# A hand-written order of tiles in a transformer block: key and value tiles in pairs, modulation tiles between them in runs of eight

## What is computed

```python
mod = silu(c) @ w_ada + b_ada            # the same with c_ctx for the context: six parts of 2048
h  = rmsnorm(x,  norm1_g) * (1 + sc1)  + sh1
hc = rmsnorm(xc, norm1_g) * (1 + csc1) + csh1
k, v   = h  @ w_in[:, K], h  @ w_in[:, V]     # K, V: 512 columns each
kc, vc = hc @ w_in[:, K], hc @ w_in[:, V]
```

## Time and profile before

| | |
|---|---|
| median of three runs | 1503.29 us |
| the profiled execution | 1502.79 us, span 1501.0 us |
| PE busy | 1467.9 us (98%) |
| DVE, ACT, POOL busy | 992.7, 666.2, 49.9 us |
| DMA | 355.73 MB, mean 237 GB/s |
| PE share of the chain that ended last | 86% |
| first 40 us | PE busy 21.72 us, DMA 371 GB/s |

### The profile page before, as it was taken

The page is one execution under the profiler, slowest core; times in us unless marked ns, Lnnn a source line. Parts: engine busy times, 40 slices in busy tenths (PEclk is TensorE's granted clock), DMA queues, the critical chain, the costliest instruction groups (busy, mean ns, idle before and its releaser), DMA issues.

```text
span 1501.0 us, 19363 instructions
## 1 busy us (share of the span) xinstructions
PE 1467.9 (98%) x7297; PEld 1208.5 (81%) x7297; DVE 992.7 (66%) x1166; ACT 666.2 (44%) x900; POOL 49.9 (3%) x32
## 2 busy tenths in 40 slices
PE   5999999999999999999999999999999999999997
PEld 2567888888888788888888888888888888888886
DVE  2456866867667679988776577777655554555456
ACT  3423444565454553344454444444444444444443
POOL 0000000101000000010100000001200000000000
PEclk9999999999999999999999999999999999999999
DMA  9997776755667679889665578778556655555552
GB/s 370 380 353 255 263 260 206 226 187 161 233 197 240 209 230 362 324 297 358 235 209 158 178 239 299 270 272 305 185 169 210 196 191 191 191 195 196 190 192 94
DMA packets 123037, 355.73 MB, mean 237 GB/s; under 512 B 10962, under 2 KB 11986, under 8 KB 122322
## 3 DMA queue, kind: packets, MB, share of 16 engines
q1 hardware_dynamic: 121492, 353.43, 69.0%
q10 hardware_dynamic: 1472, 1.31, 0.3%
HBM read 352.60 MB, written 2.10 MB: 236 GB/s over the span
## 4 chain that ended last, share of the span: by engine, by line
PE 86%; DVE 6%; issue 3%; ACT 3%; DMA 2%; ACTq 0%; POOL 0%; POOLq 0%; SPq 0%; DVEq 0%
PE bank L1546 20%; PE bank L1548 20%; PE bank L1547 20%; PE bank L1832 14%; PE bank L1835 7%; DVE wl L1116 2%; PE bank L1702 2%; PE bank L1675 1%; ACT wh L692 1%; DMA raw<-in_w_ada 1%; DVE acc L1147 1%; PE bank L1665 1%; DMA ident<-in_identity 1%; PE bank L1577 1%; DVE mx L1239 0%
## 5 line engine op out<-in xcount | busy, mean ns | idle before, releaser
L1116 DVE TENSOR_TENSOR wl<-raw,wh 128x1024 fp32r<-128x1024 f32 x451 | 555.5, 1243 | 369.1 <-ACT wh L692 367.6
L692 ACT ACTIVATE wh<-raw 128x1024 fp32r<-128x1024 f32 x452 | 473.2, 1060 | 476.3 <-PE bank L1548 282.8
L1832 PE MATMUL bank<-h2S,wh 128*128 128x512 f32 x896 | 244.8, 394 | 0.8 <-DVE wl L1116 0.7
L1546 PE MATMUL bank<-wh,hT 128*128 128x512 f32 x512 | 206.5, 403 | 1.6 <-DVE wl L1116 1.0
L1548 PE MATMUL bank<-wh,hT 128*128 128x512 f32 x512 | 200.0, 391 | 0.0
L1547 PE MATMUL bank<-wl,hT 128*128 128x512 f32 x512 | 199.7, 390 | 0.0
L1548 PE MATMUL bank<-wh,hidS 128*128 128x512 f32 x496 | 193.0, 389 | 0.0
L1547 PE MATMUL bank<-wl,hidS 128*128 128x512 f32 x496 | 193.0, 389 | 0.0
L1546 PE MATMUL bank<-wh,hidS 128*128 128x512 f32 x496 | 192.9, 389 | 0.0
L1832 PEld LDWEIGHTS bank<-h2S,wh 128*128 128x128 f32 x896 | 153.2, 188 | 21.6 <-DVE wl L1116 0.9
L1147 DVE SCALAR_TENSOR_TENSOR acc<-raw,cc,acc 128x1024 f32<-128x1024 f32 x120 | 153.5, 1279 | 0.0
(11 more groups left out here) (223 smaller groups left out, 1587.7 us busy)
## 6 DMA issues: line engine op xcount, KB each, us to landing
raw<-in_w SPq DMA_DIRECT2D x256, 512.0 KB, 3.7
raw<-in_w_ada SPq DMA_DIRECT2D x192, 512.0 KB, 5.7
raw<-in_w_in SPq DMA_DIRECT2D x128, 512.0 KB, 4.6
raw<-in_w_attn_o SPq DMA_DIRECT2D x32, 512.0 KB, 6.2
raw<-in_w_out SPq DMA_DIRECT2D x32, 512.0 KB, 5.4
raw<-in_w_fourier SPq DMA_DIRECT2D x16, 512.0 KB, 6.8
xt<-in_x SPq DMA_DIRECT2D x2, 1024.0 KB, 6.1
ct<-in_ctx SPq DMA_DIRECT2D x2, 1024.0 KB, 10.5
```

Source lines behind the costliest of these rows:

```text
L692: nc.scalar.activation(slot, raw[:, s % RAW, :], ACT.Copy).then_inc(wh_done, 1)
L1116: nc.vector.tensor_tensor(lo, raw[:, s % RAW, :], hi.bitcast(F32), ALU.subtract)\
L1546: nc.tensor.matmul(bank[b][:], a_hi, w_hi, start=first, stop=False)
L1832: nc.tensor.matmul(out[:].rearrange("p (v t) -> p v t", v=2), wh[:, slot, cols_f[f]], h2S[:, :, block, :], start=(block == 0), stop=False)
```

## The change

Seven of the sixteen entries of one table differ, the third to the ninth:

```diff
-KV_BEHIND = [18, 22, 26, 34, 36, 40, 44, 50, 52, 56, 64, 64, 64, 64, 64, 64]
+KV_BEHIND = [18, 22, 30, 30, 38, 38, 46, 46, 54, 56, 64, 64, 64, 64, 64, 64]
```

## The result

The kernel after the change takes 1507.15 us (median of ten runs, 1506.80 to 1508.27); the kernel before, on the same chip, takes 1503.35 us (ten runs, 1502.83 to 1504.27). The ratio is 1.0027 [1.0018, 1.0036], 3.8 us slower. The forecast was 1506.4 us, in a range of 1503.9 to 1508.2 us. The profiled execution of the new kernel took 1507.13 us, its span 1505.3 us, against 1502.79 and 1501.0 us of the kernel before.

What follows compares the result with a forecast made beforehand. Loads bound the first stage up to 69 us, PE after. +3.18 - 1.98 + 2 x 1.43 - 0.43 - 0.6 + 0.1 = +3.1 us on 1502.79, plus 0.5 to the median: 1506.4 us, range 1503.9 to 1508.2 us.

Steps and rivals of the forecast that it cites:

- The bound: First stage of the kernel before: bound by loads up to 69 us and by PE after it.
- run three: Eight M tiles between K1,1 and V1,0, transposes in the middle: 1.85 + 0.58 + 1.85 = 4.3 us, to 94.4 us.
- Holds at K1,0 and K2,0: PE waits for `modulate(2)` and `modulate(4)` behind the M tiles: 3.86 us chain, 2.43 us cover, 1.43 us each.
- The first run's load wait: Eight M tiles behind K0,1: PE waits 3.2 us for loads, 1.98 us before; V0,0 starts at 62.2 us.
- load 38: S2,1 before, found by PE at 67.99 us; counting five loads back put the first run's last tile at 61.2 us.
- Waits at K1,1: None expected: `modulate(3)` ready at 83 us, K1,1 wants it at 84.6 us; bounds 0 to 1.3 us.
- The sum: All legs from K0,1's end to the C3 tiles: +3.1 us, their start at 123.6 us against 120.53 us before.
- Loads late as well: Rival, 0.20: K1,1 or the eighth tile of run three or four also waits for loads; 1507.4 to 1508.4 us.
- Given back later: Rival, 0.10: a DVE backlog in the query part swallows the 3 us; not slower, 1503.3 to 1503.9 us.
- Only the runs count: Rival, 0.08: holds covered, leaving 1.0 us for three runs fewer and perhaps 2 us load wait; 1500.3 to 1502.3 us.
- the two marks of line 1079: Sign: K1,0 and K2,0 each start about 1.4 us after the last M tile, released by DVE's `hT` row.

Runs made afterwards that it cites:

- e1: Changed kernel with the transposes of S1 and S2 one tile earlier, behind four tiles of their run and not five; 1507.07 us, ratio 1.0026.
- e2: Changed kernel with V0,1 and V1,1 back behind the transposes of C1 and C2, K1 still a pair; 1504.30 us, ratio 1.0008.
- e3: Changed kernel with two M tiles in place of four between the transposes and K1,0, and the same at K2,0; 1508.81 us, ratio 1.0041.
- e4: Changed kernel with V0,0 back behind four M tiles, so the first run of eight is two of four; 1504.41 us, ratio 1.0009.
- e5: e1 with ACT's four small loads moved behind the first C3 tiles and DVE's tables into K3; 1506.72 us, ratio 1.0023.
- e6: Changed kernel with the small loads and tables moved as in e5, the odd cut left in; 1507.74 us, ratio 1.0030.
- e8: Kernel before with K1,1 moved beside K1,0 behind two M tiles and the transposes of S2 one tile earlier; 1504.08 us, ratio 1.0005.
- e9: Kernel before with K1 as the only pair, behind four M tiles, and cuts at even tiles; 1502.88 us, ratio 0.9996.
- e12: Kernel before with K1 and K2 as pairs, cuts even, and half of each S and C load from S1 on left out; 1501.49 us, ratio 0.9988.

## Why the prediction was right, point by point

**The bound.** Right but for one place. The stage waits for loads up to about 62 us now, and PE or the two holds set the pace behind it; but in run three the last tiles land so late that they would have set it, had the odd cut not (e1). All of the change's cost is inside the stage and arrives at the end.

**Holds at K1,0 and K2,0.** Forecast 2 x 1.43 us, measured 2 x 1.34. The difference is the step from DVE to PE: I had taken 0.14 us from an "issue" piece of the chain, and K1,0 starts 0.06 us behind the low half (79.36 to 79.42 us). e2 removes the holds and is faster by 2.9 us, e3 takes two tiles of cover from each and loses 1.7 us. This is shown.

**The first run's load wait.** Forecast V0,0 at 62.2 us, measured 62.69 us; the run took 7.04 us for 6.75. Its last tile could start at 61.71 in place of 61.2 us. The count back from load 38 was right for the kernel before, where the load at this place in the queue landed at 61.2 us (issued at 52.4, 8.8 us to land). In the new kernel's execution it was issued at 52.6 us and took 9.0 us: the first 0.2 us stood there before the change begins, the rest is not explained. e4 takes the wait away; forecast from the same arithmetic at 1504.6 us, it came out at 1504.41 us. Shown.

**Waits at K1,1.** V1,0 was issued at 74.89 us and landed 4.07 us later (forecast 4.0), the high half of `modulate(3)` started at 82.10 us, the low half ended at 83.5 us (forecast 83), and K1,1 began at 85.0 us with no wait. The small loads cost `modulate(3)` nothing that PE saw.

**Run three.** Wrong by 0.84 us, the one step that was mis-sized: "1.85 + 0.58 + 1.85 = 4.3 us". I had split eight tiles evenly, though the transposes stand behind the third tile of any kind after S. In the kernel before, K1,1 is one of those three, and the cut came out even; now all three are tiles of C, which makes five and three: 20 records, the transposes, 12. The rule I had read from the earlier trace rows, 0.86 us for two tiles, holds for whole pairs only. And I had counted the small loads at nothing (at 1 us in the rival), while they make the last tile of the run land 2.5 us later (94.3 in e1, 91.8 in e5; my count was 90.6). The 2 x 2 runs (e1, e5, e6) show that either is enough.

**The sum.** +3.1 us forecast, +4.22 us in the profiled execution: 0.84 us run three, 0.29 us first run, 0.23 us already there ahead of the change, less 0.17 us at the holds and 0.08 us at K/V tiles. The medians differ by 3.8 us. The error of 0.75 us in the time is smaller than the 1.1 us of the sum, and that is luck: the new kernel's profiled execution lay at its median, while I had added 0.5 us for the distance between the two. The holds and the first run's wait, which carry the sum, were forecast for the right reason.

**The rivals.** *Loads late as well* was true in part: not at K1,1, but the tiles of run three (e1 shows it), hidden behind the odd cut. *Given back later* is refuted: the delay is 4.22 us at V2,1 and 4.14 to 4.16 us up to 1062 us. *Only the runs count* is refuted by the two marks of line 1079; what it promised for fewer runs, 1.0 us for three, is borne out by e8 and e9 at 0.4 us for one, and is less than the holds cost.

## What to carry to other kernels

Before two tiles of one kind are put together, ask what stood between them as cover: here a chain of 3.8 us over ACT and DVE, hidden by 6.7 us before and by 2.4 us after, cost 1.34 us a time where a saved run and its change of tile kind bring 0.4 us. Count such a change also against the ring: while a pair runs PE frees no slot, and the run behind it has its tiles in place only as far as the ring reaches. When a test of one cause shows nothing, test it together with the other one before dropping it: of two delays side by side, taking away one shows none of its cost.

## What was not expected of the hardware

M tiles, 32 columns wide, go through PE in twos: 1.00 us for two, 1.85 for four, 2.70 for five, 2.71 for six, 1.84 for three. In e3, whose run three is cut behind the seventh tile, it is 3.56 us for seven (eight: 3.57) and 0.98 us for one. So an odd number costs as much as the next even one, and each two cost 0.86 us.

After an idle of 1.94 us PE's clock fell in two of three profiled executions (mean 0.62 and 0.67 over 44 to 48 us) and not in the third, at the same place of nearly the same program. Where it fell, K0,0 took 1.6 us longer, nearly what the smaller loads had saved. That the idle is what the fall starts from is suggested by the whole-tile kernels, which idle 0.58 or 0.59 us there and show 1.00 in all eleven profiles. It is not shown: the same idle goes without a fall in e12, and two whole-tile runs that were not profiled have the lower mean clock too.
